# A hybrid decoder step on one core: the first half of the mixer in a new order, the low halves of the weights on VectorE and GpSimd in turn, and another ending of the expert loop

## The reference, cut to what matters

```python
proj = einsum('bsd,dn->bsn', x, w_in)        # q, k, v, g_out, a_low, xr, merge
log_a = log_sigmoid(a_low @ gla_w_a2 + gla_b_a) / 16
o, s_gla_new = _gla(q, k, v, log_a, s_gla)   # 4 heads, chunks of 64 tokens, state 128 x 256 a head
o = layernorm_per_head(o) * silu(g_out)
xc = rg_conv_b + sum(conv_in[:, j:j+s] * rg_conv_w[j] for j in range(4))
r, i = sigmoid(block_diag(xc, rg_w_a) + rg_b_a), sigmoid(block_diag(xc, rg_w_x) + rg_b_x)
a = exp(-8 * r * softplus(-rg_lambda));  h = scan(a, sqrt(1 - a*a) * (i * xc), h0)
merged = gate_gla * (o @ w_branch[0]) + gate_rg * (h @ w_branch[1])
x = layernorm(ALPHA * x + merged @ w_o)
ffn = sum over the top 4 of 32 experts: weight * (clamped_swiglu(x @ w_gu[e]) @ w_down[e])
x = layernorm(ALPHA * x + ffn)
```

## Time and profile before

| what | us |
|---|---|
| three runs: lowest, median, highest | 1348.69, 1348.78, 1351.64 |
| the profiled execution's own time | 1351.2 |
| its span | 1349.4 |
| TensorE busy over the span | 1168.7 |
| GpSimd busy, nearly all of it low halves | 212.7 |
| VectorE busy | 388.6 |

### The profile page before, as it was taken

The page is one execution under the profiler, slowest core; times in us unless marked ns, Lnnn a source line. Parts: engine busy times, 40 slices in busy tenths (PEclk is TensorE's granted clock), DMA queues, the critical chain, the costliest instruction groups (busy, mean ns, idle before and its releaser), DMA issues.

```text
span 1349.4 us, 18380 instructions
## 1 busy us (share of the span) xinstructions
PE 1168.7 (87%) x7075; PEld 622.2 (46%) x7075; DVE 388.6 (29%) x642; ACT 283.3 (21%) x431; POOL 212.7 (16%) x120
## 2 busy tenths in 40 slices
PE   5996699798589999998888989898898989898894
PEld 5796687798244344333333433333333333333341
DVE  4938425643830211202021120202021120202026
ACT  3574344333411011110101111010101111010101
POOL 4664456565500000000000000000000000000000
PEclk9998899898699999999999999999999999999998
DMA  9543337552969999999999999999999999999991
GB/s 301 172 126 94 94 101 242 178 193 90 376 268 412 417 418 418 418 418 418 418 416 417 418 418 418 418 418 418 416 417 417 419 418 418 418 418 417 417 417 60
DMA packets 118385, 457.69 MB, mean 339 GB/s; under 512 B 10376, under 2 KB 49304, under 8 KB 85232
## 3 DMA queue, kind: packets, MB, share of 16 engines
q1 hardware_dynamic: 115200, 445.93, 83.2%
q0 software_dynamic: 3152, 11.31, 2.5%
HBM read 451.25 MB, written 5.95 MB: 339 GB/s over the span
## 4 chain that ended last, share of the span: by engine, by line
DMA 46%; PE 30%; SPq 11%; DVE 8%; issue 3%; ACT 3%; DVEq 0%; POOL 0%; ACTq 0%
DMA gu_w<-in_moe_w_gu 45%; PE pool L550 12%; PE pool L790 9%; SPq L405 8%; PE pool L818 3%; PE ub L759 1%; DMA dn_w<-in_w_in 1%; DVE arena L1144 1%; ACT wh L855 1%; DVE xl_most L1080 1%; PE pool L559 1%; DVE arena L1274 1%; SPq L409 1%; PE ob L802 1%; PE ub L686 0%
## 5 line engine op out<-in xcount | busy, mean ns | idle before, releaser
L790 PE MATMUL pool<-gu_w,arena 128*64 128x512 f32 x2048 | 467.2, 597 | 45.8 <-DMA gu_w<-in_moe_w_gu 45.3
L790 PEld LDWEIGHTS pool<-gu_w,arena 128*64 128x64 f32 x2048 | 138.6, 136 | 356.2 <-issue 205.4
L818 PE MATMUL pool<-dn_w,arena 128*64 128x512 f32 x1024 | 226.8, 595 | 21.6 <-ACT arena L1053 21.6
L1446 DVE TENSOR_SCALAR arena<-pool 128x512 f32<-128x512 f32 x32 | 22.1, 692 | 766.9 <-PE pool L790 766.9
L550 PE MATMUL pool<-xh,wh 128*128 128x264 f32 x576 | 175.5, 305 | 51.2 <-DVE wl L1086 12.3
L456 POOL TENSOR_TENSOR wl<-dn_w,wh 128x1024 fp32r<-128x1024 f32 x70 | 176.3, 2518 | 134.5 <-ACT wh L855 132.6
L550 PE MATMUL pool<-xh,wl 128*128 128x264 f32 x576 | 171.3, 297 | 0.0
L550 PE MATMUL pool<-xl_most,wh 128*128 128x264 f32 x504 | 150.9, 299 | 0.0
L550 PEld LDWEIGHTS pool<-xh,wh 128*128 128x128 f32 x576 | 117.5, 204 | 59.1 <-issue 41.7
L818 PEld LDWEIGHTS pool<-dn_w,arena 128*64 128x64 f32 x1024 | 70.7, 137 | 157.1 <-issue 127.9
L1051 ACT ACTIVATE arena<-arena 128x512 f32<-128x512 f32 x32 | 20.2, 630 | 486.7 <-DVE arena L1446 486.7
(11 more groups left out here) (280 smaller groups left out, 794.0 us busy)
## 6 DMA issues: line engine op xcount, KB each, us to landing
gu_w<-in_moe_w_gu SPq DMA_DIRECT2D x256, 1024.0 KB, 20.5
dn_w<-in_moe_w_down SPq DMA_DIRECT2D x256, 512.0 KB, 21.1
dn_w<-in_w_in SPq DMA_DIRECT2D x24, 1024.0 KB, 5.6
dn_w<-in_w_branch SPq DMA_DIRECT2D x8, 1024.0 KB, 5.4
gu_w<-in_state_gla POOLq DMA_DIRECT2D x8, 512.0 KB, 7.1
out_gla_sample<-gu_w POOLq DMA_DIRECT2D x8, 512.0 KB, 5.0
dn_w<-in_w_o SPq DMA_DIRECT2D x4, 1024.0 KB, 5.1
arena<-in_xT SPq DMA_DIRECT2D x2, 1056.0 KB, 6.3
```

What stands on the lines that cost most here:

```text
L790: last = mm(out, xg[:, k, j * CAP:(j + 1) * CAP], gu_w[:, k, cols], start=False, stop=(k == NB - 1))
L818: last = mm(DOWN[s * CAP:(s + 1) * CAP, :], act_t[:, k % 4, k // 4 * CAP:(k // 4 + 1) * CAP], dn_w[:, k, s * HF:(s + 1) * HF], start=(k == ...
L1446: ts(gbuf, GATE, LIMIT, None, ALU.min).then_inc(gclip, 1)
```

## The change

The code is changed in these places.

1. `mixer_jobs` and all lists that go with it: TensorE begins with `low` and `z`, then `k`, `q`, `xr`, `v0`, `v1`, the gates, `v2` to `v7`, `g`. The tiles and blocks are in the order k, q, xr, v, g. `k0` is the first projection.
2. Low halves: blocks 5, 7, ... 31 (`pool_parts`, 14 of them) on GpSimd, all 58 others on VectorE (`late_part`), each at a written place in its list. In the second half of the mixer GpSimd makes none.
3. ScalarE issues `low_w`, `a2` and `consts` from its own queue. SyncE's first four transfers of weights follow one another, and the gate weights and `b_gu` come after the fourth tile. The first four states are loaded after `kt`, `kd` and `sc` instead of at the start.
4. The convolutions are spread between the low halves. The decay of the attention is computed early, in `za`, `zb`, `eb`, `enb` at other addresses (free parts of `gu_w`).
5. The experts: 15 pairs in the loop and the last pair written out (`final`). In it the odd expert has no gather. The sum `yacc` begins as ALPHA times x instead of zero, and is multiplied by the identity into the PSUM banks of the result (`final_rows`): for 256 tokens between the last two experts, for the 8 others in the last expert. The last scatter adds onto the same banks. Statistics are read straight from PSUM, the 8 rows first. ScalarE and VectorE copy half of the last output each.

```diff
 def mixer_jobs():
-    jobs = [f"xr{n}" for n in range(NB)] + ["low"]
-    jobs += [f"k{n}" for n in range(H)]
+    jobs = ["low"] + [f"z{n}" for n in range(H)]
+    jobs += [f"k{n}" for n in range(H)] + [f"q{n}" for n in range(H)]
+    jobs += [f"xr{n}" for n in range(NB)] + ["v0", "v1"]
     for n in range(NB):
         jobs += [f"r{n}", f"i{n}"]
-    jobs += [f"q{n}" for n in range(H)] + [f"v{n}" for n in range(NB)]
-    jobs += [f"z{n}" for n in range(H)] + [f"g{n}" for n in range(NB)]
+    jobs += [f"v{n}" for n in range(2, NB)] + [f"g{n}" for n in range(NB)]
...
+        pool_parts = list(range(5, M0, 2))
...
@@ GpSimd
-            for p in range(2, NX - NB + 4):
-                low_part(p)
+            for p in pool_parts:
                 pool.wait_ge(w_hi, p + 1)
                 g.tensor_tensor(wl[p % SPLITS][:, :, :], raw_block(p), wh[p % SPLITS][:, :, :], ALU.subtract
+                                ).then_inc(w_lo_pool, 1)
+            for name in ("kt0", "kt1", "kd", "sc"):
+                wait_filled(pool, name)
+            pool.wait_ge(gla_in, 5)
             for b in range(4):
                 pool.dma_start(dstate[b] ..., state_gla[0, b] ...)
@@ ScalarE
+            sc.dma_start(low_w[:, :, :], w_in[0, :, low0:low0 + RANK].rearrange("(k p) n -> p k n", p=P)).then_inc(low_in, 16)
+            sc.dma_start(a2[:, :], gla_w_a2[0]).then_inc(a2_in, 16)
+            sc.dma_start(consts[:, :], pack).then_inc(pack_in, 16)
             for k in range(NB):
                 high_operand(k, x_raw)
-            for p in range(SPLITS):
-                high_part(p)
+            wait_filled(sc, "low")
+            nc.scalar.copy(lowT[:, :], bank("low")[0:RANK, 0:T]).then_inc(dr("low"), 1)
+            high_part(0)
             sc.wait_ge(pack_in, 16)
+            for h in range(H):
+                wait_filled(sc, f"z{h}")
+                a(zb[:, h, :], bank(f"z{h}")[:, 0:T], ACT.Abs, bias=con("b_a")[:, h:h + 1]).then_inc(z_abs, 1)
+            high_part(1)
+            high_part(2)
@@ VectorE
+            def late_part(p):
+                if p >= NSPLIT or p in pool_parts:
+                    return
+                v.wait_ge(w_hi, p + 1)
+                tt(wl[p % SPLITS][:, :, :], raw_block(p), wh[p % SPLITS][:, :, :], ALU.subtract).then_inc(w_lo, 1)
...
+            for n, done in enumerate(((), (0,), (1,), (), (2,), (3,), (4,), (5, 6, 7))):
+                late_part(11 + n)
+                for c in done:
+                    conv(c)
+            late_part(19)
+            late_part(20)
...
+            for n in range(1, NB):
+                g_gate(n)
+                late_part(27 + n)
+                me.done(scan(n - 1))
@@ TensorE, experts
+                    elif final:
+                        pe.wait_ge(gclip, n + 1)
+                        pe.wait_ge(gu_read, n + 2)
+                        for s in range(2):
+                            final_rows(FIN[2][s], s, SEQ, DEC)
...
+                    if final and j == 0:
+                        turn_weights(scat_last)
+                        for t, s in ((0, 0), (0, 1), (1, 1), (1, 0)):
+                            final_rows(FIN[t][s], s, t * P, P)
```

More of the change, by code:

```diff
@@ L163, in build @@
         vT = blocks(slot(9), NB)
[L164 to L171, removed]
+        spare = gu_w[:, 5:7, :].rearrange("p a n -> p (a n)")
+        za = blocks(slot(1, 224, HALF), H)
+        bc = za
+        zb, eb, enb = (blocks(spare[:, i * HALF:(i + 1) * HALF], H) for i in range(3))
+        qe, ke, kd = qT, enb, zb
         gT = blocks(slot(6), NB)
@@ L359, in moe_loops @@
         def moe_loops(eng, body):
-            with eng.Fori(0, PAIRS) as pair:
+            with eng.Fori(0, PAIRS - 1) as pair:
                 body(pair, pair)
@@ L365, in moe_loops @@
             with eng.If(over == 1):
-                with eng.Fori(1, PASSES) as turn:
-                    with eng.Fori(0, PAIRS) as pair:
-                        body(turn * PAIRS + pair, pair)
+                with eng.Fori(0, PASSES - 1) as turn:
+                    body(turn * PAIRS + (PAIRS - 1), PAIRS - 1)
+                    with eng.Fori(0, PAIRS - 1) as pair:
+                        body(turn * PAIRS + PAIRS + pair, pair)
+            return over * ((PASSES - 1) * PAIRS) + (PAIRS - 1)
         block = ctx.enter_context(nc.Block())
@@ L494, in _ @@
             pool.dma_start(small, outs[:, :]).then_inc(stored_early, 16)
-            for p in range(NX + 4, NX + NB + 3):
-                low_part(p)
             wait_filled(pool, "b17")
@@ L569, in _ @@
             last.then_inc(fl("low"), 1)
+            wait_drained(pe, "low")
+            pe.wait_ge(a2_in, 16)
+            for h in range(H):
+                open_job(pe, f"z{h}")
+                mm(bank(f"z{h}")[:, 0:T], a2[:, h * DK:(h + 1) * DK], lowT[:, :], start=True, stop=True
+                   ).then_inc(fl(f"z{h}"), 1)
             for n in range(H):
                 project(f"k{n}")
+            for n in range(H):
+                project(f"q{n}")
+            for n in range(NB):
+                project(f"xr{n}")
+            project("v0")
+            project("v1")
             pe.wait_ge(gate_in, 32)
@@ L774, in _, with final_rows, body @@
             pe.wait_ge(bdn_in, 16)
-            def body(it, pair):
+            def final_rows(out, s, first, rows):
+                for c in range(4):
+                    mm(out[:, c * P:(c + 1) * P], yacc[:, 4 * s + c, first:first + rows], ident[:, :],
+                       start=(c == 0), stop=False)
+            def body(it, pair, final=False):
                 for j in range(2):
@@ L879, in _ @@
                 after(f"xr{n}")
-            wait_filled(sc, "low")
-            nc.scalar.copy(lowT[:, :], bank("low")[0:RANK, 0:T]).then_inc(dr("low"), 1)
-            for h in range(H):
-                wait_filled(sc, f"k{h}")
-                nc.scalar.copy(kT[:, h, :], bank(f"k{h}")[:, 0:T]).then_inc(dr(f"k{h}"), 1)
-                after(f"k{h}")
+                if n == 0:
+                    sc.wait_ge(b_done, 2)
+                    a(zb[:, :, 0:SEQ], zb[:, :, 0:SEQ], ACT.Exp, scale=-1.0 / 16).then_inc(b_exp, 1)
+            for n in range(2):
+                evict(f"v{n}", vT[:, n, :], split_of[f"v{n}"] + SPLITS)
             for n in range(NB):
```

391 lines of the change are left out of this document (193 added, 198 removed).

## The result

| | median us | lowest to highest | ratio to before, 95% interval |
|---|---|---|---|
| before | 1348.74 | 1348.26 to 1351.64 (4 runs) | |
| changed | 1304.26 | 1302.55 to 1305.75 (4 runs) | 0.9665 [0.9647, 0.9684] |
| changed, beside other kernels later | 1302.87 | 1300.01 to 1303.46 (4 runs) | 0.9659 [0.9640, 0.9678] |

Predicted were 1311 with a range of 1299 to 1326. The gain is 44.5 us by the medians. So what is read from the two profiles adds up to some 4 us more than the medians show.

The account below looks back on a forecast made before the run. TensorE with holes was taken to bound the mixer, full DMA engines the experts from 520 us. Gains of 25.9, 9.5 and 2.5 sum to 37.9: 1313.3 from the profiled 1351.2, 1311 against the median, range 1299 to 1326.

Parts of the forecast that it names:

- the rival in which all holes go: Whole kernel: `low` starts with x, turns fall in VectorE's own waits; 49 us gained, 1300; chance 0.17.
- the likeliest case: Whole kernel: the forecast itself, 37.9 us gained, 1311 against the median; chance 0.56.
- Start: Mixer's beginning: `low` waits for x and `low_w`; `k0` begins at 19.5, between 14.9 and 24.2.
- the early end: Start of the mixer: `low` begins with x at 6, so `k0` begins at 14.9.
- the late landing: Start of the mixer: `low_w` still takes 14.2 us and lands at 15.2, so `k0` begins at 24.2.
- Blocks 0 to 17 and the convolutions: First half: VectorE has 31 us of work and turns from 51.6; gates end at 85.4 instead of 87.8.
- Blocks 18 to 31: Rest of the first half: 40.6 us of projections plus stalls; `g7` ends at 132.6 instead of 158.5.
- the slower rival: Mixer: low halves wait in VectorE's list, projections stall, 4.9 us per block; 1380 with all 14; chance 0.05.
- That turns slowed the old chain: Mixer before the change: VectorE's chain ran slowly through turns with GpSimd, four operations taking 15.06 us, 3.8 each.
- Second half: Mixer from 158.5 to 338: low halves without turns, states loaded in time; 9.5 us gained, bounds 3 and 14.
- Tail: Behind the last weights: down product 2.8 us later, 5.3 won behind it; 2.5 gained, bounds 0 and 5.
- the instruction wait that I left in the bound: Tail: the written-out last pair may cost an instruction wait on first pass; covered by bounds 0 and 5.

Follow-up runs that it names:

- low_w_sp: Changed kernel with `low_w`, `a2` and `consts` issued by SyncE behind the first tile, as before the change: 1306.22 us, ratio 0.9681 to before.
- old_all_dve2: Kernel before, old order, all low halves on VectorE, those of blocks 27 and 31 to 34 placed later than in a first try: 1329.34 us, ratio 0.9852.
- all_pool: Changed kernel with GpSimd making every low half of blocks 5 to 31 (27 instead of 14): 1313.06 us, ratio 0.9728 to before.
- old_late_dve: Kernel before with only the low halves of the mixer's second half (blocks 35 to 71) moved to VectorE: 1338.77 us, ratio 0.9924.
- old_tail_new: Kernel before with only the new ending of the experts: 1344.72 us, ratio 0.9977.
- all_dve: Changed kernel with all low halves on VectorE, none on GpSimd: 1294.98 us, ratio 0.9618 to before.
- all_dve_tail: Changed kernel without low halves on GpSimd, the sum's rows moved behind the last expert's gate and up: 1290.10 us, ratio 0.9567 to before.
- all_dve_again: Changed kernel with no low half on GpSimd, measured a second time: 1298.69 us, ratio 0.9632 to before.

## Why the prediction was right, and where its terms were off

The time came out 7 us below the forecast, inside the range, and nearer to the 1300 of the rival in which all holes go than to the 1311 of the likeliest case. In the profiles the terms were 33.8, 11.4 and 3.4, together 48.6, where I had 25.9, 9.5 and 2.5, together 37.9. Of these 10.7 us some 4 are where the two profiled executions lie beside their medians. The three terms are nearly the sizes of that rival (34, 12, 3). Its two conditions did not hold, though: `low` did not start with x (5.96) but with `low_w` (8.5), and the turns did not fall in VectorE's waits, but stood between the convolutions. The holes went in spite of them. What was right of the mechanism: the chain of recurrence and decay no longer stands bare before TensorE, VectorE and GpSimd take turns, and a microsecond out of the mixer is one out of the kernel.

- *Start.* `k0` at 17.04 instead of 19.5: 2.5 us of the miss. `low_w` took 7.7, near the early end. I had weighed the rule of the Trainium skill ("Trainium Kernel Development and Optimization", Key Constraints) as the late landing, 24.2 for `k0`. The trace agrees with the rule in part: of the 2.7 us by which `low_w` lands later in low_w_sp, 1.5 are the later issue, and 1.1 are a longer transfer. What I drew from the rule did not come. The 14.2 of the earlier trace rows were measured with four states of 512 KB issued beside it, from 4.2 to 7.4 us, whose loads the change moved away; that these were the cause was not tried by itself.
- *Blocks 0 to 17 and the convolutions.* VectorE's 31 us from 51.6 were 29.4 from 50.4. The four turns cost 1.9, 2.0, 2.0 and 2.2 (2.29 for 0.43, twice 3.09 for 1.07, 3.40 for 1.22), 8.1 where I had 9.6; the small waits and half clock that I added behind were not there (the granted clock is 1.00 from 60 to 90 us). TensorE is through the gates at 81.0 instead of 85.4: 1.9 more of the miss.
- *Blocks 18 to 31.* This is the term that was most mis-sized: `v7` held 1.8, `g3` 1.0, a half clock 2.5 and an instruction 1.3, 6.6 in all. From 81.0 to 124.8 it is 43.7 for 40.6 of work, where I had 47.2. Two thirds of what is lost are the three waits for low halves shown above (0.21, 1.18 and 0.69). `g3` is one of them, with 1.18; `v7` is not held, the clock stays at 1.00, and no run shows the late instruction. A lead of two projections takes up most of a turn, as I had written against the slower rival, and I should have used it for the forecast. With these 3.5 the miss of the first half is 7.9.
- *That turns slowed the old chain* was half the truth: old_all_dve2 shows 9 of the 18 us of holes gone without them. The new order, with all that goes with it, is worth 23 (all_pool against old_late_dve, 0.9924 - 0.9728, less the ending) to 27 us.
- *Second half.* 9.5 predicted, 10.2 by old_late_dve, 11.4 in the profiles. The states come in time, `b1` and `wo` wait 1.1 less each as said. `b13` waits 1.6 instead of 1, for ScalarE's high half.
- *Tail.* 2.5 predicted, 3.1 by old_tail_new, 3.4 in the profiles. The first expert's product began at 378.37 and now at 332.99, 45.4 earlier; against that the last gate and up ends 4.8 later (I had 3.9), the down product 4.1 later (2.8), and behind it 7.3 are won (5.3). At the entry of the last pair stands a wait of 3.3, which I take for the instruction wait that I left in the bound (see the last section). How much of it lies on the path stays open; behind it the chain names no wait for weights any more, ahead of it there were such waits.
- *The slower rival's* price was 4.9 us for a block. From all_pool to all_dve it is 18 by the medians and 15 by the ratios for 27 blocks, 0.5 to 0.7 each. The rule of the Trainium skill behind it ("SBUF — State Buffer", Who interferes with whom) is borne out as to blocking: 3.09 for 1.07. What made the price small is that the next projection mostly did not wait.

The account by experiments, in shares of 1348 us: second half 10.2, ending 3.1, 13 low halves moved to VectorE in the first half 8.9 (0.9728 - 0.9662); the rest of the 45.6, 23.4, is the order. It is the rest, so that the sum says nothing of its own. It also holds six blocks (2 to 4 and 32 to 34) that all_pool has on VectorE and old_late_dve on GpSimd, and it takes for granted that the parts add up, which no run shows.

## What to carry to other kernels

When a helper engine takes turns with the one whose chain is waited for, try giving the chain's engine all of the work: 1.2 us in its own list can be cheaper than 2.5 us beside it plus a turn of 2. Put what a long chain needs first in the order of the bounding engine, and see that no drain stands behind an operation that waits for the product which needs the drained bank. At the end of a kernel, products that need no late input belong in the waits for the last activation and the last copies, not ahead of the last large product.

## What the runs showed that I had not expected

- A loop body written out once more comes with a wait of 3.3 to 4.4 us on TensorE at its entry in every kernel with the new ending (3.31 changed, 3.50 old_tail_new, 4.12 all_dve_tail, 4.39 all_dve_again), none in the kernel before. The profile names no releaser. I read it as a wait for instructions, which is argued and not tried: in the changed kernel no other engine's work ends where it ends, and one instruction transfer of 16 KB falls into it in each of the four, while the kernel before has none from 1100 to 1300 us. In the changed kernel the gate and up behind it takes 15.45 instead of 13.76, at a granted clock of 0.89.
- Not every wait without a releaser is of that kind. Those of 0.21, 1.18 and 0.69 in the first half looked the same in the table of waits, and only the ends of the low halves, set beside them, tell what they were.
- TensorE's granted clock fell to 0.50 behind the waits for the drains in the old order, but not behind the single waits of 0.7 and 1.2 in the new one: the stretch from 90 to 132 is granted 1.00.
